# Sums of squares for two output norms: five additions on VectorE, three mean products on TensorE where there were eight

## The reference

```
o_sb = stick_breaking_attention(qh, kh, to_heads(v))
...
o_rg = rg_lru(x_rg, ...) * jax.nn.gelu(g_rg)
mixed = jnp.concatenate(
    [rms_norm_2(o_sb, out_norm_sb[l]), rms_norm_2(o_rg, out_norm_rg[l])], axis=-1)
x = x + jnp.einsum('bse,ed->bsd', mixed, w_out[l])
```

## Time and profile before

| | |
|---|---|
| runs (3), median | 3236.73 us |
| lowest and highest run | 3233.26 and 3238.44 us |
| the profiled execution | 3237.41 us |
| its span | 3235.6 us |
| TensorE matmul busy | 3180.0 us (98%) |
| VectorE busy | 1994.8 us (62%) |
| ScalarE busy | 1289.7 us (40%) |
| GpSimd busy | 1380.9 us (43%) |

### The profile page before, as it was taken

The page is one execution under the profiler, slowest core; times in us unless marked ns, Lnnn a source line. Parts: engine busy times, 40 slices in busy tenths (PEclk is TensorE's granted clock), DMA queues, the critical chain, the costliest instruction groups (busy, mean ns, idle before and its releaser), DMA issues.

```text
span 3235.6 us, 44771 instructions
## 1 busy us (share of the span) xinstructions
PE 3180.0 (98%) x15336; PEld 2731.7 (84%) x15336; DVE 1994.8 (62%) x3048; ACT 1289.7 (40%) x1945; POOL 1380.9 (43%) x674
## 2 busy tenths in 40 slices
PE   6999999999999999999999899999999999999999
PEld 4888888888888888888887678999999998888887
DVE  5553386522665063611219769898868697888887
ACT  3222343223332142422224664345747473333333
POOL 3444435444544444444444534466434343223221
PEclk8999999999999999999999899999999999999999
DMA  6554326532554222232322203356899989999997
GB/s 258 193 191 166 124 93 209 192 122 87 188 200 164 98 91 97 80 108 92 105 97 72 78 16 126 104 173 206 297 358 302 357 296 348 345 343 347 348 343 258
DMA packets 219995, 620.71 MB, mean 192 GB/s; under 512 B 22624, under 2 KB 88416, under 8 KB 217312
## 3 DMA queue, kind: packets, MB, share of 16 engines
q1 hardware_dynamic: 89296, 324.76, 29.3%
q10 hardware_dynamic: 93712, 160.11, 14.1%
q0 software_dynamic: 36864, 134.23, 11.8%
HBM read 572.88 MB, written 46.14 MB: 191 GB/s over the span
## 4 chain that ended last, share of the span: by engine, by line
PE 40%; issue 36%; POOL 18%; DVE 4%; ACT 1%; POOLq 0%; DMA 0%; ACTq 0%; DVEq 0%
POOL wlo L552 18%; PE bank L1794 6%; PE bank L1796 6%; PE bank L1795 6%; PE bank L2298 5%; PE bank L2297 5%; PE bank L2299 5%; PE bank L2256 3%; DVE qrstd L1426 1%; PE bank L2102 1%; PE bank L2206 0%; DVE cx L1448 0%; DMA ring<-u_rows_dram,cell_u 0%; DVE o L1465 0%; PE bank L2279 0%
## 5 line engine op out<-in xcount | busy, mean ns | idle before, releaser
L552 POOL TENSOR_TENSOR wlo<-raw,whi 128x1024 fp32r<-128x1024 f32 x386 | 993.6, 2577 | 1148.3 <-ACT whi L599 1147.2
L1794 PE MATMUL bank<-hhi,whi 128*128 128x512 f32 (+1 forms) x2672 | 991.1, 371 | 1.8 <-POOL wlo L552 1.8
L1795 PE MATMUL bank<-hlo,whi 128*128 128x512 f32 (+1 forms) x2672 | 983.4, 368 | 0.0
L1796 PE MATMUL bank<-hhi,wlo 128*128 128x512 f32 (+1 forms) x2672 | 983.4, 368 | 0.0
L599 ACT ACTIVATE whi<-raw 128x1024 fp32r<-128x1024 f32 x599 | 631.4, 1057 | 878.1 <-PE bank L1796 532.1
L1794 PEld LDWEIGHTS bank<-hhi,whi 128*128 128x128 f32 x2672 | 501.8, 188 | 67.9 <-issue 4.2
L1795 PEld LDWEIGHTS bank<-hlo,whi 128*128 128x128 f32 x2672 | 501.9, 188 | 64.7 <-issue 1.2
L1796 PEld LDWEIGHTS bank<-hhi,wlo 128*128 128x128 f32 x2672 | 501.6, 188 | 64.4
L1079 DVE CUSTOM_DVE_ANT_0 ada_raw<-ada_raw,cond_row 128x1024 f32<-128x1024 f32 x128 | 309.6, 2450 | 157.9 <-DMA ada_raw<-ada_dram 157.8
L1616 DVE TENSOR_TENSOR wlo<-raw,whi 128x1024 fp32r<-128x1024 f32 x213 | 260.5, 1223 | 144.8 <-ACT whi L599 144.4
L580 POOL DMA_INDIRECT ring<-u_rows_dram,cell_u x128 | 201.8, 1576 | 254.9 <-DVE dots L1628 236.4
(11 more groups left out here) (341 smaller groups left out, 3981.5 us busy)
## 6 DMA issues: line engine op xcount, KB each, us to landing
raw<-stream_dram SPq DMA_DIRECT2D x599, 512.0 KB, 3.4
ada_raw<-ada_dram ACTq DMA_DIRECT2D x128, 512.0 KB, 4.0
expert_acts<-act_out ACTq DMA_DIRECT2D x128, 192.0 KB, 4.7
act_in<-expert_acts ACTq DMA_DIRECT2D x128, 192.0 KB, 6.0
expert_weights<-spread ACTq DMA_DIRECT2D x16, 1024.0 KB, 11.8
g_ring<-expert_weights ACTq DMA_DIRECT2D x128, 128.0 KB, 5.3
first_raw<-ada_dram SPq DMA_DIRECT2D x8, 1024.0 KB, 18.3
x<-xin_dram ACTq DMA_DIRECT2D x1, 2048.0 KB, 4.7
```

The lines of the kernel that those rows point to most:

```text
L552: pool.tensor_tensor(wlo[:, s, :, :], raw[:, s, :, :], whi[:, s, :, :].bitcast(F32), ALU.subtract).then_inc(lo_ready, 1)
L1794: pe.matmul(bank, whi[:, s, b, :], rhi, start=start, stop=False)
L1795: pe.matmul(bank, whi[:, s, b, :], rlo, start=False, stop=False)
L1796: return pe.matmul(bank, wlo[:, s, b, :], rhi, start=False, stop=stop)
```

## The change

One more tile, `out_sq_next`, takes the squares whose number isn't a multiple of four. VectorE gets five additions `out_sq += out_sq_next`: for the squares 1, 2 and 3 (iterations 4, 6, 8), 5 (iteration 18) and 6 (iteration 23), each behind the `w_hi` of the iteration. Of the mean products, one over the added squares of the rg half stands at the end of TensorE's iteration 10. Two stand behind the third group of the output product: one over the added squares 4, 5 and 6, and one over square 7, which is not added. The semaphore `out_sq_added` takes the place of `out_sq_used` ahead of most squares. The copy of the rg mean moves from ScalarE's iteration 10 to 11.

```diff
-MEAN_COPY_AT = 10
+MEAN_COPY_AT = 11
...
+def squares_added(j):
+
+    return sum(1 for i in range(j) if i % CT and i < KT - 1)
...
+    out_sq_next = place("out_sq_next", 94, [P, T], F32)
...
-                if j:
-                    act.wait_ge(out_sq_used, j)
-                act.activation(out_sq[:, :], o[:, k, :], ACT.Square).then_inc(out_sq_ready, 1)
+                if j == CT:
+                    act.wait_ge(out_sq_used, 1)
+                elif j > 1:
+                    act.wait_ge(out_sq_added, squares_added(j))
+                act.activation(out_sq[:, :] if j % CT == 0 else out_sq_next[:, :], o[:, k, :], ACT.Square).then_inc(out_sq_ready, 1)
...
                 if u == MEAN_COPY_AT:
-                    act.wait_ge(out_sq_used, CT)
+                    act.wait_ge(out_sq_used, 1)
...
-                act.wait_ge(out_sq_used, CT if half else KT)
+                act.wait_ge(out_sq_used, 1 if half else 3)
...
+            def add_out_square(j):
+                dve.wait_ge(out_sq_ready, j + 1)
+                if squares_added(j):
+                    dve.wait_ge(out_sq_added, squares_added(j))
+                dve.tensor_tensor(out_sq[:, :], out_sq[:, :], out_sq_next[:, :], ALU.add).then_inc(out_sq_added, 1)
...
                 if u >= LAG:
                     round_weights(u - LAG)
+                if u - 1 in OUT_AT:
+                    j = OUT_ORDER.index(OUT_AT[u - 1])
+                    if j % CT:
+                        add_out_square(j)
...
                 if u < len(UNITS) + LAG:
                     round_weights(u - LAG)
+                if u == len(UNITS) + LAG - 1:
+                    add_out_square(KT - 2)
...
-            def sum_out(j):
-
-                pe.wait_ge(out_sq_ready, j + 1)
-                pe.matmul(psum[7][:, :], sq_plain[:, MEAN_H, :], out_sq[:, :], start=j % CT == 0, stop=j % CT == CT - 1).then_inc(out_sq_used, 1)
+            def sum_out(n):
+
+                if n < 2:
+                    pe.wait_ge(out_sq_added, (CT - 1, KT - 3)[n])
+                else:
+                    pe.wait_ge(out_sq_ready, KT)
+                squares = out_sq_next if n == 2 else out_sq
+                pe.matmul(psum[7][:, :], sq_plain[:, MEAN_H, :], squares[:, :], start=n < 2, stop=n != 1).then_inc(out_sq_used, 1)
...
-                if u - 2 in OUT_AT:
-                    sum_out(OUT_ORDER.index(OUT_AT[u - 2]))
+                if u == MEAN_COPY_AT - 1:
+                    sum_out(0)
...
                     for g in range(2):
                         out_rest(psum[RG_BANK[g]][:, :], g, 0)
-                    sum_out(KT - 2)
...
             rg_part(2)
-            sum_out(KT - 1)
+            sum_out(1)
+            sum_out(2)
```

More of the change, by code:

```diff
@@ L371, in build @@
     out_sq_used = sem("out_sq_used")
+    out_sq_added = sem("out_sq_added")
     out_std_ready = sem("out_std_ready")
```

## The result

The changed kernel takes 3240.13 us, median of 22 runs (3231.95 to 3247.77), the kernel before 3236.91, median of 22 (3231.88 to 3244.18). The ratio is 1.0014, with a 95% interval of 1.0008 to 1.0020. So it is slower, by 3.2 us between the medians and by 4.5 us by the ratio, inside the 0.2% that I had called no change. But the interval excludes no change and the 1.1 us of gain that the sum forecast. The median lies at the upper end of my range (3240.3), and 1.0014 on the 3236.73 of the runs before would be 3241.3, just beyond it.

The account below looks back on a forecast made before the run. TensorE was taken as the bound: time it gains to the norm nearly counts in full. TensorE's path at -0.9 us plus a vanished 0.24 wait gave -1.1 against 3237.41, or 3236.3; median 3235.6, range 3231.3 to 3240.3.

Parts of the forecast that it names:

- The sum of the small terms: Attention stage of the second block to the norm: removed products, additions and waits together give -1.1 us; forecast given 60%.
- The weighted product of unit 5: Near 1881 us: TensorE gets there at -2.3 us but waits for w_lo, which is shifted by only -1.6.
- the idle time of 0.24 at the norm: Norm behind the mixer: TensorE's 0.24 us wait for VectorE's last sum of squares was to disappear.
- the predicted wait of the last weighted product for w_lo: Near 1930 us: w_lo ends 0.45 us later beside the fifth addition, so 0.29 us is gained instead of 0.8.
- The two paths: At the norm: VectorE's path at -1.76 us, TensorE's at -0.9 after 0.86 for the product moved behind.
- late fall: Rival, gap between 1914 and 1919 us: the clock falls in the widened gap, +0.6 in all, 3237.3 us; 12%.
- The order at the shared port: At each addition behind w_hi: VectorE goes first without delay, and GpSimd's w_lo beside it ends 0.45 us later.
- GpSimd first: Rival at each addition: GpSimd's w_lo goes first, VectorE is through 0.54 us after it; 3236.9 us in all; 13%.
- the clock's rise at 1863.6: Early attention stage: TensorE's clock was taken to rise from 0.50 to 1.00 at 1863.6 us, as before.
- the clock does not rise at 1863.6: Rival: with less TensorE work the lower level stays; 14 iterations cost 36 us, 3272 us in all; 2%.
- the removed sixth product: Iteration 19: no gain, TensorE already waits for unit 16's w_lo; removal adds 0.9 us of idleness before the gap.
- the first product: Iteration 3: TensorE already waits 0.37 us for VectorE's ab_lo behind it, so removing it gains nothing.

Follow-up runs that it names:

- e1: The changed kernel as it stands, run again beside the kernel before; ratio to before 1.0010.
- e2: The changed kernel with three products over constants put back at iterations 3, 5 and 7, additions kept; ratio to before 0.9988.
- e3: The changed kernel with two products over constants put back at iterations 14 and 19 alone; ratio to before 1.0014.
- e5: The kernel before with five of its eight products only 16 columns wide and no additions; ratio to before 1.0016.
- e9: The kernel before with only products 0, 1 and 2 (iterations 3, 5, 7) 16 columns wide, no additions; ratio to before 1.0016.
- e11: The changed kernel with 4 and 8 filler matmuls in the two waits for w_lo (iterations 20 and 21); ratio to before 1.0012.
- e4: The changed kernel with all five products put back over constants, additions kept; ratio to before 0.9999.
- e6: The kernel before with five additions over constants on VectorE, all eight products kept; ratio to before 1.0003.
- e10: The kernel before with only products 4 and 5 (iterations 14 and 19) 16 columns wide; ratio to before 0.9998.
- e12: The changed kernel with products put back at iterations 3, 5 and 7 plus filler matmuls in iterations 20 and 21; ratio to before 1.0002.
- e16: Repeat of the changed kernel with three products put back at iterations 3, 5 and 7; ratio to before 1.0005.
- e17: The changed kernel with four rounded 512-column matmuls in place of each product at iterations 3, 5 and 7; ratio to before 1.0003.
- e8: The changed kernel with 32 filler matmuls, 16 ahead of unit 2's scores and 16 behind unit 4's; ratio to before 0.9995.
- e15: The changed kernel with one product over constants put back at iteration 7; ratio to before 1.0015.
- e14: The changed kernel with one product over constants put back at iteration 5; ratio to before 1.0005.
- e13: The changed kernel with one product over constants put back at iteration 3; ratio to before 1.0009.
- e7: The kernel before with 32 filler matmuls, 16 ahead of unit 2's scores and 16 behind unit 4's; ratio to before 0.9995.
- e18: The changed kernel with 32 filler matmuls in the two early waits and products put back at iterations 5 and 7; ratio to before 0.9989.

## Why the prediction was wrong, point by point

**The sum of the small terms held.** Where the clock rose early, the steps can be checked. w_lo of units 0, 5, 16 and 19 in e1, the changed kernel:

```profile
1855.87 1.66 POOL L579 TENSOR_TENSOR w_lo<-w,w_hi 128x512 fp32r<-128x512 f32 x1 [16.48 <-DVE w_hi L1501]
...
1875.65 1.29 POOL L579 TENSOR_TENSOR w_lo<-w,w_hi 128x512 fp32r<-128x512 f32 x1 [2.02 <-DVE w_hi L1501]
...
1913.91 1.71 POOL L579 TENSOR_TENSOR w_lo<-w,w_hi 128x512 fp32r<-128x512 f32 x1 [2.27 <-DVE w_hi L1501]
...
1926.43 1.67 POOL L579 TENSOR_TENSOR w_lo<-w,w_hi 128x512 fp32r<-128x512 f32 x1 [2.08 <-DVE w_hi L1501]
```

Unit 0 to 5: 19.78 us against 21.59, a gain of 1.8 where I had 1.6. The weighted product of unit 5 stood right at the end of its w_lo (1876.99 and 1875.65 + 1.29), as forecast. Unit 5 to 16: 38.26 against 37.99, a loss of 0.27 where I had 0.13. Unit 19 to the norm: 47.34 against 46.75, a loss of 0.6 where I had 0.33. The difference is the idle time of 0.24 at the norm, which I had counted as a wait that would go. It stands in the profiles of all the kernels. Here it is in e2, whose end is that of the changed kernel with the product that moved behind, beside the predicted wait of the last weighted product for w_lo:

```profile
1927.93 0.50 PE L2138 MATMUL bank<-w_hi,v_hi 128*128 128x512 f32 x1 [0.31 <-POOL w_lo L579]
...
1973.53 0.70 PE L1888 MATMUL bank<-sqsum,mean_d 128*128 128x512 f32 x1 [0.24 <-DVE sqsum L1120]
```

The two paths that I had added up apart, TensorE's and VectorE's, are one. In the changed kernel VectorE waits for TensorE's last output group before it makes the last sum of squares:

```profile
1978.09 0.69 DVE L1561 TENSOR_TENSOR out_part<-bank,out_rstd 128x512 f32<-128x512 f32 x1 [0.63 <-PE bank L2173]
```

From TensorE's first matmul behind that group (1970.27 before, 1977.89 changed) to the norm's mean product it is 4.94 and 4.93 us. Where TensorE comes later, the sum of squares does too, and the 0.24 stay.

So with the clock rising early and no late fall, the sum is -1.8 + 0.3 + 0.6 = -0.9 against the forecast's -1.1. This is put together from one profile, without its late fall; no run had exactly this course.

**The order at the shared port held.** VectorE came first in five of five, the additions took 0.68 and w_lo 0.4 more. The rival "GpSimd first" did not occur. This also agrees with the rule of the Trainium skill ("SBUF — State Buffer", "Who interferes with whom"): the first to start holds it, the other waits.

**The step that failed is the clock's rise at 1863.6.** The sum took the clock's course as unchanged. I had the mechanism as a rival, "the clock does not rise at 1863.6", and gave it 2%, with two arguments from rows: no product lies in the 5.8 us ahead of the rise, and none in the 16 us from 1879 at 1.00. Both rows are right and neither bears on it. The second tells that the upper level is kept without products, not that it is reached. The first looked at one stretch ahead of one rise of one execution. Of the six profiles with the three early products gone and the early waits unfilled (the changed kernel, e1, e3, e5, e9, e11), in four the clock stayed at the lower level for 37.5 us and in two (e1, e9) for 17; of the eight with the three products or the same amount of work in place (before, e2, e4, e6, e10, e12, e16, e17), all rose after 17 to 20.5 us, by about 1864. The mean clocks of the runs say the same: 38 of 79 at 0.989 or less, against none of 77. A trace of before shows one draw, and the change moved the odds. What decides between two executions of one kernel stays open.

**Its price was wrong the other way.** I had 36 us, the lower level for all 14 iterations. Between w_lo of unit 0 and of unit 5 it lasts 17 us longer and costs 7.0: the stretch took 26.82 us in the changed kernel's profile and 19.78 in e1. It took 26.8 to 27.4 in the four profiles with the long lower level, and 19.7 to 21.8 in the thirteen with the early rise and no fill ahead of it. With -0.9 for the rest and 1.5 for a late fall, a loss of 3 to 4.5 us comes out if something like every second run misses the early rise. That share is an estimate from the medians, the four of six and the 38 of 79; the two halves of the 22 runs, 7.3 us apart, fit it.

**The range.** The median lies inside it by luck. Its upper end, 3240.3, was built of GpSimd first and the late fall on top of the highest run, and not of the clock's late rise.

**The late fall.** I had it at 12% and 1.7 us. Where it came, units 16 to 19 took 1.5 us more in six profiles, 2.0 in e8 and 3.0 in e15. It was the removed sixth product that I made responsible, and e3 and e9, which have it and fell, speak against that.

**What was hidden.** Of the first product I had said that TensorE already waits behind it, "so nothing is gained". The wait grew from 0.37 to 2.18 us, idle time that is free by the chain of waits. It may be part of what the clock answered to, but it isn't enough by itself: e14, which still has this wait of 2.18, rose early in its profile and had no run at 0.989 or less. e13, with the first product back, had two, and its ratio of 1.0009 doesn't tell it from the changed kernel or from before with certainty.

## What to carry to other kernels

Work of TensorE in a stretch where its clock is at the lower level isn't worth only its time: taken away, it can delay the rise, and here seventeen microseconds more at half the clock cost more (7.0 us) than five products of 0.9. Before such work is moved to another engine, look at where the granted clock rises behind each idle stretch, in more than one execution, and give the clock's rise a rival with a chance that one trace can't refute. Where the effect of a change is one or two per mille, compare the mean clock of the runs together with their times: here it set the kernels apart, while the single profiles of e1 and e9 happened to show an early rise. And before a fill is called useless, look at what it delays: in e7 the clock gave 2.9 us and the fill took 3.2.

## What the runs showed of the hardware

TensorE can be busy without a gap and stay at the lower clock. In the changed kernel, in a mix of matmuls of 64 and 128 rows and of 128 to 512 columns:

```profile
1858.00:1880.00 22.00, 22.00 (x79) 0.50 0.00 1
```

The ends of matmuls in a trace are modelled, so small gaps between them needn't show. The Trainium skill ("TensorE: Matmul & The Clock Gate", "What's actually happening") says that a sustained stretch of activity ends the lower level. This trace doesn't agree: where the early waits had no fill, the lower level lasted 17 to 20.5 us or 37.5. Both occurred in the same kernel, with the same idle times of TensorE ahead (3.77, 2.18 and 0.69 us in the changed kernel's profile and in e1's), so what these traces show of its work doesn't tell which it will be.

Filler matmuls in a wait don't settle what comes behind them: in e7 the clock fell at 1848 between the two fills and rose at 1855 in the second, in e8 the lower level came at 1855 behind both and lasted 17 us, in e18 with two more products 7 us. In the stretch from unit 0 to 5, where TensorE is busy all the time, the clock's price is plain in both directions: about 6 us less at the lower level gave 2.9 us (e7), 17 us more cost 7.0.
